# An encoder trunk of two layers: output products of stage B in pairs, PSUM emptied one step later, reciprocals widened on ScalarE

## What is computed

```python
for l in range(DEPTH):                       # DEPTH = 2
    h = rms_norm(x, pre_norm_g[l])
    if l % 2 == 0:                           # layer 0: A and B side by side
        qa, ka, va, qb, kb, vb, ga, gb = split(h @ w_in_ab)
        ya = diff_attention(qa, ka, va, ...)       # 4 heads of 2 x 64, all earlier chunks
        yb = sliding_window_gqa(qb, kb, vb, sinks) # 8 heads of 64, 2 kv heads, 2 chunks of 64
        y = concat([ya * silu(ga), yb * silu(gb)]) @ w_out_ab
    else:                                    # layer 1: C
        qc, kc, vc, gc = split(h @ w_in_c)
        yc = chunked_relpos_attention(qc, kc, vc, rel_bias)  # 16 heads of 64, 9 chunks
        y = (yc * silu(gc)) @ w_out_c
    x = x + rms_norm(y, post_norm_g[l])
```

## Time and profile before

| | us |
|---|---|
| median of 3 runs | 1394.42 |
| lowest, highest | 1393.45, 1396.52 |
| the profiled execution | 1392.36 |
| its span in the trace | 1390.4 |
| PE, matmuls | 1234.1 busy (89%) |
| DVE | 891.2 busy (64%) |
| ACT | 580.6 busy (42%) |
| POOL | 389.3 busy (28%) |

### The profile page before, as it was taken

The page is one execution under the profiler, slowest core; times in us unless marked ns, Lnnn a source line. Parts: engine busy times, 40 slices in busy tenths (PEclk is TensorE's granted clock), DMA queues, the critical chain, the costliest instruction groups (busy, mean ns, idle before and its releaser), DMA issues.

```text
span 1390.4 us, 17337 instructions
## 1 busy us (share of the span) xinstructions
PE 1234.1 (89%) x6480; PEld 1043.0 (75%) x6480; DVE 891.2 (64%) x1789; ACT 580.6 (42%) x1271; POOL 389.3 (28%) x280
## 2 busy tenths in 40 slices
PE   6999999999878877768568999999999999998863
PEld 6978888888766665656457888888888888886652
DVE  5575857677576676765444386766847586675667
ACT  5544434434333434433333444444444354443332
POOL 4322131231423334433722212213230222312002
PEclk9999999999999999889779999999999999999976
DMA  6341020110211122222211111102110211111302
GB/s 197 107 127 61 16 62 16 35 42 16 62 46 46 48 78 91 91 76 61 91 61 46 51 46 50 46 16 65 31 65 16 65 31 50 46 35 31 121 31 91
DMA packets 86243, 82.07 MB, mean 59 GB/s; under 512 B 3184, under 2 KB 74864, under 8 KB 86160
## 3 DMA queue, kind: packets, MB, share of 16 engines
q1 hardware_dynamic: 86160, 80.97, 18.6%
HBM read 72.52 MB, written 13.68 MB: 62 GB/s over the span
## 4 chain that ended last, share of the span: by engine, by line
PE 74%; DVE 13%; ACT 5%; issue 4%; POOL 2%; DMA 1%; SPq 0%; POOLq 0%; DVEq 0%; ACTq 0%
PE dense L926 38%; PE dense L933 13%; PE pv_ps L1004 8%; PE scores L1078 6%; PE turned L1048 5%; PE dense L901 3%; DVE e_sb L1410 2%; DVE y L1387 2%; DVE rec_wide L1449 1%; DVE pT_lo L1474 1%; ACT e_sb L1176 1%; DVE yT_lo L1530 1%; PE dense L960 1%; ACT pT_hi L1205 1%; PE turned L1036 1%
## 5 line engine op out<-in xcount | busy, mean ns | idle before, releaser
L926 PE MATMUL dense<-hT_hi,w_hi 128*128 128x512 f32 x880 | 354.8, 403 | 0.0
L926 PE MATMUL dense<-hT_lo,w_hi 128*128 128x512 f32 x880 | 348.5, 396 | 0.0
L926 PE MATMUL dense<-hT_hi,w_lo 128*128 128x512 f32 x880 | 347.9, 395 | 0.0
L1176 ACT ACTIVATE e_sb<-e_sb,low 128x256 f32<-128x256 f32 (+7 forms) x256 | 170.7, 667 | 371.3 <-DVE low L1410 371.3
L799 POOL TENSOR_SCALAR w_hi<-w_f 128x1024 fp32r<-128x1024 f32 x90 | 102.0, 1133 | 793.2 <-PE dense L926 663.7
L802 POOL TENSOR_TENSOR w_lo<-w_f,w_hi 128x1024 fp32r<-128x1024 f32 x90 | 219.7, 2441 | 7.5
L926 PEld LDWEIGHTS dense<-hT_hi,w_lo 128*128 128x128 f32 x880 | 167.8, 191 | 37.7
L926 PEld LDWEIGHTS dense<-hT_lo,w_hi 128*128 128x128 f32 x880 | 168.6, 192 | 28.9
L926 PEld LDWEIGHTS dense<-hT_hi,w_hi 128*128 128x128 f32 x880 | 168.4, 191 | 29.2
L1474 DVE TENSOR_TENSOR pT_lo<-turned,pT_hi 128x640 fp32r<-128x640 f32 (+3 forms) x224 | 133.7, 597 | 55.7 <-ACT pT_hi L1205 52.7
L933 PE MATMUL dense<-w_hi,yT_hi 128*128 128x512 f32 x256 | 111.0, 434 | 62.6 <-DVE y L1387 43.6
(11 more groups left out here) (128 smaller groups left out, 1789.5 us busy)
## 6 DMA issues: line engine op xcount, KB each, us to landing
w_f<-in_w_in_c SPq DMA_DIRECT2D x36, 512.0 KB, 4.0
w_f<-in_w_in_ab SPq DMA_DIRECT2D x34, 512.0 KB, 3.9
w_f<-in_w_out_ab SPq DMA_DIRECT2D x12, 512.0 KB, 3.6
rel_tiles_dram<-rel_rows_dram SPq DMA_DIRECT2D x1, 5120.0 KB, 23.1
bias<-rel_tiles_dram SPq DMA_DIRECT2D x8, 640.0 KB, 5.3
y<-in_x SPq DMA_DIRECT2D x8, 512.0 KB, 7.7
xs<-in_x SPq DMA_DIRECT2D x8, 512.0 KB, 3.6
x_dram<-y SPq DMA_DIRECT2D x8, 512.0 KB, 4.1
```

The lines of the kernel that those rows point to most:

```text
L926: last = mm(dense[:, x.n % 2, :], lhs[:, d * P:(d + 1) * P], rhs[:, d, x.f * HALF:(x.f + 1) * HALF], start=i == 0, stop=i == 23)
L1176: copy(e, e, ACT.Exp, scale=-1.0, bias=stat_col(low, it.j), accum_out=stat_col(total, it.j)).then_inc(s_exp, 1)
```

## The change

Eleven things change. PE's order within a step stays as it was: uses of the bank, projection, product with v, transposes, scores.

- B's outputs go in pairs. The rows of two units are gathered in one bank by six matmuls and emptied once, one use in a step; only the last pair has two in a step. For this the second unit's weights have places of their own (hi_place, lo_place: o_hi over vT, o_lo over bias, and parts of hT).
- A bank filled in a step is emptied by DVE and ACT in the next step, and there first; in steps 16 to 19 of A's and C's units the projections are still emptied in the same step, last.
- A step has one use of dense 2 after the projection, or one before and one after; none at its end.
- DVE's order in a step: the last step's bank, `lowest`, `lo_of_turned`, and then the others. Before, `lo_of_turned` came first.
- For deferred units the transposes come 2 steps after the item, and not 3. For B the product with v comes 2 steps after the transposes, with two sets of pT places (`pT_set`).
- The reciprocal is taken over 128x4 on DVE, and ACT spreads it (`widen`).
- A3's outputs spread over 11 steps and not 6; C6's over 16, one a step, and not 6.
- Projections: q of C0 moves into B7, the first half of v of C1 into the first four steps of C0, the second half of v of C7 into C7; q of a B unit comes before the gate of the one before.
- C0 gets a step without an item (160), so C1 to C7 start a step later; TOTAL is 320 and not 322.
- In the norm, rows 1, 2, 6 and 7 start one step earlier; for rows 4 and 5 the transposes come one step later against their start; rows 6 and 7 get places of their own (`x_place`).
- C7's last outputs use two banks and not three, and start one step earlier.

The core of the diff:

```diff
+    def step(self, j):
+
+        return self.start + j + (1 if self.kind == "C" and self.i == 0 and j >= 8 else 0)
...
-            g_ = Turned("p", u_, -1, it_.step + 3, item=it_, first=ITEMS[-2] if u_.kind == "A" else it_)
+            g_ = Turned("p", u_, -1, it_.step + (2 if u_.deferred else 3), item=it_, first=ITEMS[-2] if u_.kind == "A" else it_)
...
             if t_ % 2:
-                pv_ = Pv(u_, h_, t_ - 1, len(PVS), g_.step + 1, g_)
+                pv_ = Pv(u_, h_, t_ - 1, len(PVS), g_.step + (2 if u_.kind == "B" else 1), g_)
...
-                        GATES.append(Gate(u_, len(GATES), it_.step + 6, slice(c_, c_ + 2 * P), pv_, len(RECS) - 1))
+                        GATES.append(Gate(u_, len(GATES), pv_.step + 2, slice(c_, c_ + 2 * P), pv_, len(RECS) - 1))
...
-    segment([("g", B[i_], f_)] + ([("q", B[i_ + 1], B[i_ + 1].half)] if i_ < 7 else []), B[i_].start, B[i_].start + 7)
-segment([("q", C[0], 0), ("k", C[0], 0), ("v", C[0], 0), ("g", C[0], 0)], C[0].start - BRIDGE, C[0].start - 1)
-segment([("q", C[0], 1), ("k", C[0], 1)], C[0].start + 8, C[0].start + 8)
-segment([("v", C[0], 1)], C[0].start + 9, C[0].start + 10)
-segment([("g", C[0], 1)] + both("v", C[1]), C[0].start + 11, C[0].start + 15)
+    gate_, query_ = ("g", B[i_], f_), ("q", B[i_ + 1], B[i_ + 1].half) if i_ < 7 else ("q", C[0], 0)
+    segment([query_, gate_] if i_ < 7 else [gate_, query_], B[i_].start, B[i_].start + 7)
+c_ = C[0].start
+segment([("k", C[0], 0), ("v", C[0], 0), ("g", C[0], 0)], c_ - BRIDGE, c_ - 1)
+segment([("v", C[1], 0)], c_, c_ + 3)
+segment([("k", C[0], 1), ("q", C[0], 1)], c_ + 8, c_ + 8)
+segment([("v", C[0], 1)], c_ + 9, c_ + 9)
+segment([("g", C[0], 1)], c_ + 10, c_ + 11)
+segment([("v", C[1], 1)], c_ + 12, c_ + 16)
...
+segment(both("g", C[6]) + [("v", C[7], 0)], c_, c_ + 15)
+segment([("k", C[7], 0), ("q", C[7], 0)], c_ + 16, c_ + 19)
+c_ = C[7].start
+segment([("k", C[7], 1), ("q", C[7], 1)], c_, c_ + 3)
+segment([("v", C[7], 1)], c_ + 4, c_ + 5)
+segment([("g", C[7], 0)], c_ + 6, c_ + 7)
+segment([("g", C[7], 1)], c_ + 8, c_ + 9)
...
+    f_.tail = any(u_.in_tail(f_.step) and f_.step < u_.step(20) for u_ in UNITS if u_ is not C[7])
+    f_.drain = f_.step if f_.tail else f_.step + 1
...
-    s_ = B[i_].start + 13
-    out_steps(B[i_], [(s_, 2), (s_ + 1, 2), (s_ + 2, 2), (s_ + 3, 2)])
+    SPARE_RAW.append((A[i_ + 1].start + 1, "sum", (A[i_],), 0, 0))
+    out_steps((A[i_],), even_plan(A[i_ + 1].start + 3, 16, 17))
+SPARE_RAW.append((B[0].start + 1, "sum", (A[3],), 0, 0))
+out_steps((A[3],), [(B[0].start + 3 + t, 1 + t % 2) for t in range(11)])
+for i_ in range(0, 6, 2):
+    s_ = B[i_ + 1].start + 8
+    out_steps((B[i_], B[i_ + 1]), [(s_ + t, 1) for t in (3, 4, 6, 7, 8, 9, 11, 12)])
 s_ = C[0].start
-out_steps(B[7], [(s_ - 5, 2), (s_ - 4, 2), (s_ - 1, 2), (s_, 2)])
+out_steps((B[6], B[7]), [(s_ - 5, 2), (s_ - 4, 2), (s_ - 1, 2), (s_, 2)])
...
-out_steps(C[6], [(s_ + 3, 3), (s_ + 4, 3), (s_ + 5, 3), (s_ + 6, 3), (s_ + 7, 2), (s_ + 8, 2)])
-NORM = [B[5].start + 1, B[5].start + 5, B[6].start + 1, B[6].start + 5,
-        C[0].start - 3, C[0].start - 2, C[0].start + 1, C[0].start + 2]
+out_steps((C[6],), [(s_ + 4 + t, 1) for t in range(16)], (2, 3, 4, 5, 6, 7, 0, 1))
+NORM = [B[5].start + 1, B[5].start + 4, B[6].start, B[6].start + 5,
+        C[0].start - 3, C[0].start - 2, C[0].start, C[0].start + 1]
 for r_, a_ in enumerate(NORM):
...
+    EARLY_AT[s_], LATE_AT[s_] = (uses_[:1], uses_[1:]) if len(uses_) > 1 else ([], uses_)
...
-    s_ = C[7].start + 4 * k_ + 11
+    s_ = C[7].start + 4 * k_ + 10
...
+    def pT_set(pv):
+
+        return 3 * (pv.n % 2) if pv.u.kind == "B" else 0
...
+    def x_place(r):
+
+        if r < 6:
+            return xs[:, r % 2, :]
+        return x_hi[:] if r == 6 else w_f32[:, 3, :]
...
-        def out_matmuls(bank, cols, w, w_l):
-            for n, (lhs, rhs) in enumerate(((yT_hi, w), (yT_hi, w_l), (yT_lo, w))):
-                last = mm(bank, lhs[:, cols], rhs, start=n == 0, stop=n == 2)
+        def out_matmuls(bank, parts):
+            for m, (c, w, w_l) in enumerate(parts):
+                for n, (lhs, rhs) in enumerate(((yT_hi, w), (yT_hi, w_l), (yT_lo, w))):
+                    last = mm(bank, lhs[:, c:c + P], rhs, start=m == n == 0, stop=m == len(parts) - 1 and n == 2)
             return last
...
         for s in range(TOTAL):
-            uses = SPARES_AT.get(s, [])
-            early = uses[:-1][:1] if uses else []
-            late = uses[len(early):]
-            for x in early:
+            for x in EARLY_AT[s]:
                 spare_use(x)
             project(*PROJ_AT.get(s, (0, 0)))
-            for x in late[:1]:
+            for x in LATE_AT[s]:
                 spare_use(x)
-            for r, _, p in recs_at(s, 4):
+            for r, p in RECS_AT[s]:
                 turn_rec(r, p)
             for p in PVS_AT[s]:
                 times_v(p)
                     turn(x)
...
-                if new(s_pv, pv.n):
-                    act.wait_ge(s_pv, pv.n)
+                if new(s_pv, pv.n - (1 if pv.u.kind == "B" and pv.n > 16 else 0)):
...
+        def widen(r, it):
+
+            if new(s_drec, r + 1):
+                act.wait_ge(s_drec, r + 1)
+            if new(s_rturn, r):
+                act.wait_ge(s_rturn, r)
+            copy(rec_wide[:].rearrange("p (o h a) -> p h o a", o=2, h=2),
+                 stat_col(rec, it.j - 3, 4).rearrange("p (h o a) -> p h o a", h=2, a=1).broadcast_to([P, 2, 2, HD]),
+                 ACT.Copy).then_inc(s_rwide, 1)
...
+            for x in LATE_AT.get(s - 1, []):
+                if x.what == "turn":
+                    hi_of_rows(x)
             for x in TURNED_AT[s - 1]:
                 hi_of_turned(x)
+            for it in ITEMS_AT.get(s - 1, []):
+                exp(it)
+            for x in EARLY_AT[s]:
+                if x.what == "turn":
+                    hi_of_rows(x)
+            for p in PVS_AT.get(s - 1, []):
+                out_low(p)
+            for x in FILLS_AT[s]:
+                if not x.tail:
+                    hi_of_fill(x)
             for u in A:
...
-            nc.vector.reciprocal(rec_wide[:].rearrange("p (o h a) -> p h o a", o=2, h=2),
-                                 src.rearrange("p (h o a) -> p h o a", h=2, a=1).broadcast_to([P, 2, 2, HD])).then_inc(s_drec, 1)
-
-        def times_rec(r, it, p):
+            nc.vector.reciprocal(stat_col(rec, it.j - 3, 4), src).then_inc(s_drec, 1)
...
         for s in range(TOTAL):
+            for x in LATE_AT.get(s - 1, []):
+                spare_use(x)
+            for it in ITEMS_AT.get(s - 1, []):
+                lowest(it)
             for x in TURNED_AT[s - 1]:
                 lo_of_turned(x)
-            for it in ITEMS_AT.get(s - 1, []):
-                lowest(it)
+            for x in EARLY_AT[s]:
+                spare_use(x)
             for it in ITEMS_AT.get(s - 2, []):
                 if not it.u.deferred:
                     normalise(it)
-            for r, it, _ in recs_at(s, 2):
+            for r, it in DENOMINATORS_AT[s]:
                 denominators(r, it)
+            for p in PVS_AT.get(s - 1, []):
+                out_sum(p)
+            for r, p in RECS_AT[s - 1]:
+                times_rec(r, p)
             if s == 1:
                 constants()
+            for x in FILLS_AT[s]:
+                if not x.tail:
+                    lo_of_fill(x)
             for g in GATES_AT[s]:
                 gated(g)
             for g in GATES_AT.get(s - 1, []):
                 gated_lo(g)
-            uses = SPARES_AT.get(s, [])
-            early = uses[:-1][:1]
-            for x in early:
-                spare_use(x)
-            for x in FILLS_AT[s - 1]:
-                if x.b == "g":
-                    lo_of_fill(x)
-            for x in FILLS_AT[s]:
-                if x.b in "kq":
-                    lo_of_fill(x)
-            for x in uses[len(early):]:
-                spare_use(x)
-            for _, n, row, half, _ in LAST_AT[s]:
+            for _, n, row, half, _ in LAST_AT.get(s - 1, []):
                 last_out(n, row, half)
-            for p in PVS_AT[s]:
-                out_sum(p)
-            for r, it, p in recs_at(s, 5):
-                times_rec(r, it, p)
             for r in norm_rows(s, 1):
                 if new(n_yr, r + 1):
```

269 lines of the change are left out of this document (152 added, 117 removed).

## The result

The kernel before took 1393.93 us in the median (1392.30 to 1396.52, 4 runs), the changed kernel 1316.60 (1313.51 to 1317.95, 4 runs). The ratio is 0.944, with a 95% interval of 0.9417 to 0.9464. So the change is faster by 77 us, and 1316.6 lies above the range of 1250 to 1310. The profiled execution took 1317.74 us, its span is 1316.0.

A forecast was written before the change was run, and what follows sets the result against it. PE was taken as the bound, with about 200 of 1390 us waits; savings of 74.6 + 17.8 + 10.5 + 5.1 + 16.6 + 0.2 = 124.8 took 1392.36 to 1267.6, plus 2.06 for the median: about 1270, range 1250 to 1310.

The forecast's parts named there:

- B, forecast -74.6: Stage B, steps 80 to 148: 230 us instead of 304.6, with PE becoming the bound, nearly as in C.
- what I leave as waits: Stage B: 22 us of PE waits left, 10 at norm rows, 7 in single steps, 5 at the stage's start and end.
- It should vanish: Stage B: PE's 1.48 us wait for pT_lo should go with earlier transposes and a later product with v.
- The bridge, forecast -17.8: Norm and bridge, steps 149 to 159: 37 us instead of 54.8, the end set by a chain through POOL.
- behind it ... about 5: Bridge, behind POOL's queue: last row's scaling, its transposes and two emptyings, about 5 us.
- The 53 us: Bridge's time if all fifteen roots and splits each lost a DVE pass of 1.1 us, 16 us on top.
- 3 us of waits: Steps 160 to C1: waits added to 69.0 us of PE work, giving 72.0 instead of 82.5.
- it fits with 0.3 us to spare: A and C1 to C5: DVE's new order needs 1.6 of 1.91 us between scores and product with v; no change.
- The sign that the prediction set for it: C5 over 79 us, or a product with v that waits for pT_lo there, would show the prediction wrong.
- the thin cover fails a little: Rival: 0.2 to 0.5 us lost in the 220 steps of A and C, 1310 to 1390 us; chance 0.08.
- PE at the low clock in the bridge: Rival: bridge's 26.7 us of PE work takes up to 53, some 10 standing out; 1280 us, chance 0.08.
- B stays bound by latency (1294): Rival: fixed engine orders without slack lose 0.4 us in each of 60 steps of B, 24 us; chance 0.22.

The follow-up runs named there:

- e2: Changed kernel with POOL's weight-split subtraction in steps 80 to 159 run over 32 of 1024 columns, so output isn't the reference's; ratio 0.9304 to the kernel before.
- e3: Changed kernel with the outputs of pairs B0+B1, B2+B3 and B4+B5 starting one step later; ratio 0.9401 to the kernel before.
- e12: Changed kernel plus six edits: step-160 emptying, later paired outputs, moved splits, sum before v's passes, two bridge banks, rows 0 to 3 spread; 1287.59 us, ratio 0.9232.
- e15: Kernel e12 with B's transposes back to three steps behind the scores and the product with v one step behind them; ratio 0.9275 to the kernel before.
- e8: Changed kernel with B's transposes back to three steps behind the scores and the product with v one step behind them; ratio 0.9428 to the kernel before.
- e10: Changed kernel with the second half of rows 4 to 7's transposes put in another bank in the bridge; ratio 0.9392 to the kernel before.
- e14: Kernel e12 with C0's second-half k and q splits behind the norm's last root, and rows 4 to 7's additions of x on DVE; ratio 0.9234.
- e1: Changed kernel with k and q of C0's second half emptied at the end of step 160 instead of in step 161; 1306.43 us, ratio 0.9393.
- e9: Changed kernel with the last step's product with v emptied before the transposed v, from C1 on; ratio 0.9374 to the kernel before.
- e16: Kernel e12 with DVE making pT_lo before lowest in A and C1 to C6, as in the kernel before; ratio 0.9261.

## Why the prediction was wrong

- **B, forecast -74.6, measured -58.8.** The accounting of parts held: ACT's widening copy took 0.42 us (0.4 forecast), and DVE's busy time in B is 149.0 without the lock (153 forecast). The step that failed is "what I leave as waits", 22 us. It was derived from DVE's share of the window (74%) and from undisturbed durations. The mutual lock of POOL and DVE was weighed only for the bridge; in B it cost 20.6 us in e2's profiled execution. And the paired outputs were taken as free to start, though their yT_lo had one step of slack instead of the three steps that single outputs had. With one step more B came to 229.1 (e3), and to 229.8 with the other edits (e12). That is close to the forecast, but not a proof of its list: the norm's rows cost 13 us in e12, not 10.
- **Earlier turns.** "It should vanish" was right for the wait; the part is worth 4 us (e15), and nothing while step 99's wait was there (e8).
- **The bridge, forecast -17.8, measured -2.1.** POOL's queue ended after 37.2 us, just where I put the end of the whole. The terms had left it 32 (26 + 1 + 5), so 5 us were missed before that. The larger failed term is "behind it ... about 5": it was 15.5. I had priced the last row's emptyings, and not the queue of halves through one bank, each behind DVE's and ACT's other work. e10 gives 5.0 us of the bridge to the bank, e2 3.6 to the lock with the splits, and moving the additions (e14) 3.5 to 4 more, by the lock or by DVE's shorter pass. The 53 us that the prediction names for lost passes at every root and split is met by the 52.7 measured, but by chance: taking away the splits' lock gave 3.6 us and moving the additions at most 4 more, not 16; the roots' part was not tested. What sets the remaining 44.7 us is not settled; the waits of 3.8 us before row 5's transposes and 2.8 before step 158's product with v are its largest.
- **160 to C1, forecast -10.5, measured -0.7.** The failed step is "3 us of waits". An item-less step gives k and q time to be emptied, but their emptying stood in step 161 behind transposes. e1 got 6.4 back with one line.
- **A and C, forecast 0, measured 3.1 + 5.4 longer.** Here "it fits with 0.3 us to spare" failed. The sign that the prediction set for it came: C5 took 79.5 us, over 79. The rival of a thin cover that fails a little was real in kind and small: a wait for pT_lo in one step of a unit. In C4:

```profile
1006.24 0.39 PE L1085 MATMUL pv_ps<-pT_hi,v_st 128*128 128x256 f32 x1 [0.17 <-DVE pT_lo L1567]
```

  The tenth step is 0.4 us longer than before. Another 0.5 to 0.6 us a unit come from the sum behind v's passes (e9), a move in DVE's order that the prediction didn't price. With the old order of lowest and pT_lo (e16) A got 1.6 us back and C nothing.
- **C6, forecast -5.1, measured -1.0.** The work did shrink; a wait of 1.9 us for yT_lo in step 276 and one of 0.7 for y in step 280 took part of its place.
- **C7 up to step 303, -16.6,** came out to the tenth, with eleven steps of the kernel before set against ten of the changed one, in the forecast as in the measurement. **The end,** forecast -0.2, gave 3.7; no run looked for the cause.
- The rival "the thin cover fails a little" had a span of times, 1310 to 1390, that holds the result, but its mechanism gave 8.5 us at most of the 50 that the stretches miss. That the time fell into its span is luck. "PE at the low clock in the bridge" wasn't it either: the clock was 0.79 there, but PE was busy in 35.2 of 52.7 us and waited for rows and banks. The rival "B stays bound by latency (1294)" named the mechanism nearest to what happened in B, but as a loss spread over 60 steps, and most of it was two steps and three rows.

## What to carry to other kernels

In a kernel like this one, a fixed order of several engines is decided by single operations, not by shares of a window: for each thing that PE waits for, count the steps between producer and consumer, and ask whether the slowest duration of the producer in the trace fits, not the usual one. When a change brings outputs nearer to what makes them, give a step of slack back. And where the last wait goes to an engine that does several rows in turn, price the whole queue behind it.

## What the runs showed of the hardware

**A lock hits the smallest operations as hard as the large.** DVE's addition over 128x4 takes 0.15 us and took 2.28 at 466.70 in the changed kernel (POOL subtracts from 466.58 to 468.97) and 2.13 in e12. Passes with one input in PSUM kept their durations beside POOL: y over 128x512 took 0.67 to 0.69 us in all its 128 runs in the changed kernel, hT_lo 0.69 in all 16. The Trainium skill, "SBUF — State Buffer", section "Who interferes with whom", says that a DVE instruction with two SBUF inputs and a GpSimd one that reads SBUF exclude each other for the whole instruction, while one with at most one SBUF input, outside the 2-port modes, doesn't take part. The trace agrees, with these numbers.

**The same program meets the lock at different places.** In the changed kernel the gate was hit; in e1, with the same orders up to there, POOL had got its weights earlier against DVE, and the lock fell on the 4-wide addition:

```profile
412.78 1.63 DVE L1540 TENSOR_TENSOR den<-total,sink_e 128x4 f32<-128x4 f32 x1
...
414.54 0.41 DVE L1618 SCALAR_TENSOR_TENSOR o_sb<-o_sb,gate 128x256 f32<-128x256 f32 x1
...
417.13 0.69 DVE L1624 TENSOR_TENSOR yT_lo<-o_sb,yT_hi 128x256 fp32r<-128x256 f32 x1
```

PE waited 1.55 us at step 99, not 4.09, and B took 238.4 us instead of 245.8. POOL follows the arrival of a DMA (its split of B0's output weights began at 407.37, in the changed kernel at 408.83), DVE follows PE. I take this for the reason that executions of one kernel lay 7 us apart in e3 and up to 12.7 in e9 (1306.54 to 1319.22), and those of e12, which has slack at this place, only 2 us (1287.03 to 1289.17); that reason is argued from two traces, not shown by a run of its own.

**A wait costs twice.** After its waits of 3.3 to 4.9 us PE's matmuls of 512 columns were 0.42 us apart in the changed kernel. From the first output matmul of step 99 to the next step PE took 5.1 us, at a granted clock of 0.50, and in e2, where the wait is gone, 2.8; in step 115 it was 5.3 against 2.8. So each of these two waits cost some 2.4 us beside itself, twice the 1.1 of the expectations. Over B the granted clock was 0.94 in the changed kernel and 1.00 in e12.
